# Mod jobs one turn later, fetches and exponentials in another order, and Hyena's inverse transform folded over even and odd times

## The chip, the cores and the metric

One NeuronCore of a Trainium2 chip runs the whole program. The metric is device microseconds of one execution, median of several runs. TensorE does the matrix products; VectorE, ScalarE and GpSimd (called Pool) run beside it, and the SyncE and Pool queues start the DMA transfers. Engines wait for each other through counting semaphores.

## The reference, cut to what matters

A two-layer diffusion backbone on 256 latent tokens of width 1024 with 256 context tokens. Layer 0 mixes with neighbourhood attention and a short convolution, layer 1 with a Hyena long convolution. Each layer has a SwiGLU FFN before and after the mixer, and each sub-layer takes shift, scale and gate from `silu(c) @ w_mod`.

```python
def half_step_ffn(x, g_pre, g_post, shift, scale, gate, w_gate, w_up, w_down):
    h = modulated_norm(x, g_pre, shift, scale)
    y = (jax.nn.silu(h @ w_gate) * (h @ w_up)) @ w_down
    return x + FFN_RES * gate * rms_norm(y, g_post)

def bidirectional_long_conv(u, h_fwd, h_bwd):
    n = u.shape[1]
    k = jnp.concatenate([h_fwd, jnp.zeros((1, HY_WIDTH), jnp.float32), h_bwd[1:][::-1]], axis=0)
    u_f = jnp.fft.rfft(u.astype(jnp.float32), n=2 * n, axis=1)
    k_f = jnp.fft.rfft(k, n=2 * n, axis=0)
    y = jnp.fft.irfft(u_f * k_f[None], n=2 * n, axis=1)[:, :n]
    return y.astype(u.dtype)

# hyena_mixer
    x0, x1, v = jnp.split(short_conv(h @ w_in, short_w), 3, axis=-1)
    u = v * x1
    return (x0 * (bidirectional_long_conv(u, h_fwd, h_bwd) + u * bias)) @ w_out
```

Sizes: D = 1024, D_FF = 2816, 256 tokens, depth 2.

## The kernel before

Every engine has a program of its own, written out by hand, and its order is the order of that text.

**Weights.** The stream `wstream` is cut into units of 128x1024 f32 (512 KB), fetched by SyncE into a ring of six slots. ScalarE rounds a unit to `whi` (`split_hi`, L652), VectorE subtracts to get `wlo_r` (`split`, L1106), four units ahead of TensorE (LEAD = 4). A product is three matmuls: hi by hi, lo by hi, hi by lo (L1798 to L1800 with columns, L1879 to L1881 in down projections).

**FFN.** There are four, numbered 0 to 3; FFN 0 carries the context tokens too. Each has 11 turns of six units: gate and up of pair 0 (k = 0, 1), gate and up of pair 1 (k = 2, 3), two down units (k = 4, 5). After unit 1 and after unit 3 ScalarE takes `silu` (L789), VectorE multiplies (`gate_up`, L1323) and makes `act_lo` (`act_los`, L1328), for which the down units wait. Turns are written out, except for ranges in `LOOPS`, which are loops. `at_steps` puts other calls at a turn and a k.

**Jobs.** The modulation `silu(c) @ w_mod` runs as jobs on VectorE beside the FFN turns: eight multiply-adds of 128x512 (`job_ops`, L1121, L1123), a hi part by ScalarE (`job_hi`), a lo part (`job_lo`, L1133), and in the turn after it two matmuls by TensorE (`job_sum`). FFN 1 has six jobs, FFN 2 eight, FFN 3 two. Pool fetches their 2 MB in four parts (`load_job`), each after the multiply-adds that free its place (`steps_before`). `batch_rows`, `batch_columns` and `batch_out` turn the finished rows into columns; `gate_out` finishes a gate.

**Start.** The first four loads of `w_mod` (16 chunks) are computed ahead on TensorE: `chunk_hi` by ScalarE (L880), `chunk_lo` by VectorE (L1442), `ahead` by TensorE (L1991, L1993; L1984 for load 3), then `row` (L888), `ahead_columns` (L2002) and `ahead_out` (L1153). `warm_bank` issues matmuls of the identity whose result nobody reads (L1972).

**Filters.** In turns 6 to 10 of FFN 1 Hyena's filters are made: `filter_layer`, `sine_argument` (L1658 to L1668 on VectorE), `sine` on ScalarE, `filter_out`, `filter_sums`. They need `w4`, `window` and `bias_row`; the transforms after FFN 1 need `dft`.

**Attention.** Projection units 0 to 23 (`take_out`, L943 to L948 on ScalarE; `short_conv`, L1511 to L1522 on VectorE), beside them the context's norm (`spread`, L1190 and L1216; its transposes L1865 stand behind unit 9). Then per head: `score`, `maxima` (L1531), `exps` (L984), `normalise` (L1561, L1563), transposes (L2199), copies to `prob_t` (L1006), `values` (L2187).

**Hyena.** Projection units 0 to 23: ScalarE takes a tap (L1071), VectorE the two others (`taps`, L1731, L1734), then a split, then what stands in the tables. The spectrum of `u` comes from TensorE (`u_spectrum`, L2324); `spectrum_product` multiplies it on VectorE in `YF_STEPS` steps for each half g of the channels, placed by `YF_AT` (unit to list of (g, step)). `yf_step` counts the steps. The inverse transform (`inverse`, L2337) takes the 128 channels of chunk c: four f32 matmuls of 256 columns, each in two records. Inverses 0 to 3 stand behind projection units 19 to 22 (`IV_AT`), inverses 4 to 7 behind units 1 to 4 of the output projection (`IV_UNITS`). Inverses 0 and 4 wait for all steps of their half. `inverse_out` (L1745, L1747) and `mixed_hi` (L1063) follow.

## Time and profile before

| what | us |
|---|---|
| median of 3 runs | 1323.95 (1320.19 to 1324.26) |
| profiled execution | 1324.37 |
| its span, first to last instruction | 1322.7 |
| TensorE busy | 1292.2 (98%) |
| VectorE busy | 988.4 (75%) |
| ScalarE busy | 637.8 (48%) |
| granted TensorE clock, mean | 0.995 |

Stages in the profiled execution, from its timeline: start 0 to 60, FFN 0 to 368 with the context's down projection to 434, attention to 581, FFN 1 from 589, FFN 2 from 801, Hyena from 1003, FFN 3 from 1128, end at 1322.7. Times below are microseconds from the start of the span. A line of the timeline or chain starts with its start and its length; `xN` is a count of instructions; in brackets stands how long the engine had been idle and what ended it. A matmul's end is modelled, about 0.28 to 0.40 after its start, while the next one starts 0.117 (256 columns of f32r) or 0.235 (512) after it.

### The profile page before, as it was taken

How to read it: one execution, taken by the hardware profiler on the slowest of the kernel's cores; microseconds unless marked ns; L12 is line 12 of the kernel's file. 1: busy time of each engine (PE TensorE's matmuls, PEld its weight loads, DVE VectorE, ACT ScalarE, POOL GpSimd, SP SyncE). 2: the span in 40 equal slices, each digit the busy share in tenths (PEclk: the TensorE clock that was granted, in tenths of full speed). 3: DMA queues.
4: the chain of work that ended last, by engine and by line, in shares of the span. 5: the costliest groups of instructions: out<-in, count | busy, mean ns of one | idle time of the engine just before them, and what ended most of it. 6: DMA issues, size and time to landing. Idle time of an engine off the chain costs nothing.

```text
span 1322.7 us, 21457 instructions
## 1 busy us (share of the span) xinstructions
PE 1292.2 (98%) x7746; PEld 1111.7 (84%) x7746; DVE 988.4 (75%) x1459; ACT 637.8 (48%) x1011; POOL 119.9 (9%) x211
## 2 busy tenths in 40 slices
PE   7999999999999999999999999999999999999998
PEld 5678777887778998688998888989998988999997
DVE  5688777788786886758786768888768887965554
ACT  6533333233376665765444447444447434644444
POOL 2100010111100422011110000111000000000000
PEclk9999999999999999999999999999999999999999
DMA  9655657777755754259886546898654536656553
GB/s 357 210 175 177 203 203 241 257 240 254 242 172 177 221 145 110 81 178 335 286 303 203 176 145 207 303 354 287 215 182 142 159 125 205 222 180 189 184 184 109
DMA packets 76474, 275.67 MB, mean 208 GB/s; under 512 B 9274, under 2 KB 9829, under 8 KB 75760
## 3 DMA queue, kind: packets, MB, share of 16 engines
q1 hardware_dynamic: 52128, 187.00, 43.5%
q0 software_dynamic: 24272, 87.65, 19.6%
q8 instruction: 50, 0.82, 0.2%
q14 instruction: 24, 0.20, 0.1%
HBM read 273.57 MB, written 1.05 MB: 208 GB/s over the span
## 4 chain that ended last, share of the span: by engine, by line
PE 80%; DVE 9%; ACT 5%; DMA 3%; issue 2%; POOL 0%; DVEq 0%; ACTq 0%; SPq 0%; POOLq 0%
PE gu L1798 16%; PE gu L1800 16%; PE gu L1799 15%; PE acc L1879 8%; PE acc L1881 8%; PE acc L1880 8%; DVE wlo_r L1106 3%; DMA area<-in_wmod_dram 2%; DMA wlo<-in_wstream_dram 1%; ACT whi L652 1%; DVE part L1123 1%; DVE x_lat L1307 1%; PE acc L2164 1%; PE acc L2166 1%; PE acc L2165 1%
## 5 line engine op out<-in xcount | busy, mean ns | idle before, releaser
L1798 PE MATMUL gu<-h_hi,whi 128*128 128x256 f32 (+1 forms) x1664 | 510.6, 307 | 2.2 <-ACT area L948 1.2
L1800 PE MATMUL gu<-h_hi,wlo_r 128*128 128x256 f32 (+1 forms) x1664 | 507.6, 305 | 0.0
L1799 PE MATMUL gu<-h_lo,whi 128*128 128x256 f32 (+1 forms) x1664 | 507.4, 305 | 0.0
L1106 DVE TENSOR_TENSOR wlo_r<-wlo,whi 128x1024 fp32r<-128x1024 f32 x350 | 420.9, 1222 | 84.5 <-ACT whi L652 82.4
L652 ACT ACTIVATE whi<-wlo 128x1024 fp32r<-128x1024 f32 x350 | 360.7, 1050 | 81.0 <-DMA wlo<-in_wstream_dram 80.6
L1798 PEld LDWEIGHTS gu<-h_hi,whi 128*128 128x128 f32 x1664 | 313.4, 188 | 26.5 <-issue 4.5
L1799 PEld LDWEIGHTS gu<-h_lo,whi 128*128 128x128 f32 x1664 | 313.3, 188 | 18.9 <-issue 0.7
L1800 PEld LDWEIGHTS gu<-h_hi,wlo_r 128*128 128x128 f32 x1664 | 313.9, 189 | 15.7
L1123 DVE SCALAR_TENSOR_TENSOR part<-wm,cvec,part 128x512 f32<-128x512 f32 x266 | 199.4, 750 | 7.0 <-DVE part L1123 0.5
L1879 PE MATMUL acc<-whi,act_hi 128*128 128x512 f32 x440 | 177.6, 404 | 5.6 <-DVE act_lo L1328 5.1
L1881 PE MATMUL acc<-wlo_r,act_hi 128*128 128x512 f32 x440 | 174.0, 396 | 0.0
L1880 PE MATMUL acc<-whi,act_lo 128*128 128x512 f32 x440 | 174.0, 395 | 0.0
L546 POOL DMA_DIRECT2D wm<-in_wmod_dram x128 | 68.0, 532 | 749.6 <-DVE part L1123 576.0
L1879 PEld LDWEIGHTS acc<-whi,act_hi 128*128 128x128 f32 x440 | 82.9, 188 | 30.1 <-DVE act_lo L1328 8.1
L789 ACT ACTIVATE gated<-gu 128x256 f32<-128x256 f32 x66 | 25.3, 383 | 171.0 <-PE gu L1800 171.0
L1881 PEld LDWEIGHTS acc<-wlo_r,act_hi 128*128 128x128 f32 x440 | 83.0, 189 | 20.9
L1880 PEld LDWEIGHTS acc<-whi,act_lo 128*128 128x128 f32 x440 | 83.1, 189 | 17.5
L1323 DVE TENSOR_TENSOR act<-gated,gu 128x256 f32<-128x256 f32 x66 | 27.7, 420 | 80.7 <-ACT gated L789 80.6
L786 ACT ACTIVATE total_hi<-part 128x512 fp32r<-128x512 f32 x38 | 24.0, 632 | 78.9 <-DVE part L1123 78.6
L847 ACT ACTIVATE act_hi<-act 128x256 fp32r<-128x256 f32 x22 | 9.2, 418 | 104.1 <-DVE act L1415 104.1
L1328 DVE TENSOR_TENSOR act_lo<-act,act_hi 128x256 fp32r<-128x256 f32 x88 | 37.2, 423 | 20.4 <-ACT act_hi L793 16.4
L793 ACT ACTIVATE act_hi<-act 128x256 fp32r<-128x256 f32 x66 | 27.6, 418 | 48.7 <-DVE act L1323 48.7
(375 smaller groups left out, 1251.1 us busy)
## 6 DMA issues: line engine op xcount, KB each, us to landing
wlo<-in_wstream_dram SPq DMA_DIRECT2D x350, 512.0 KB, 3.6
wm<-in_wmod_dram POOLq DMA_DIRECT2D x132, 512.0 KB, 5.6
area<-in_wmod_dram POOLq DMA_DIRECT2D x11, 512.0 KB, 19.9
z<-in_gate_rows_dram POOLq DMA_DIRECT2D x6, 512.0 KB, 9.6
gate_keep<-in_gate_rows_dram POOLq DMA_DIRECT2D x5, 512.0 KB, 8.0
area<-in_rpb_dram POOLq DMA_DIRECT2D x32, 64.0 KB, 3.5
x_lat<-in_x_in_dram SPq DMA_DIRECT2D x1, 1024.0 KB, 7.8
area<-in_ctx_in_dram SPq DMA_DIRECT2D x1, 1024.0 KB, 9.0
```

The lines of the kernel that those rows point to most:

```text
L546: pool.dma_start(wm[:, 2 * part_:2 * part_ + 2, :], src[:, 2 * part_:2 * part_ + 2, :]).then_inc(wm_landed[part_ // 2], 16)
L652: nc.scalar.activation(whi[:, phase % RING, :], raw[:, phase % RING, :], ACT.Copy).then_inc(hi_done, 1)
L1106: nc.vector.tensor_tensor(wlo[:, u.base % RING, :], raw[:, u.base % RING, :], whi[:, u.base % RING, :].bitcast(F32), ALU.subtract).then_in ...
L1123: ins = nc.vector.scalar_tensor_tensor(out=part[:, :], in0=wm[:, kt, :], scalar=c, in1=part[:, :], op0=ALU.mult, op1=ALU.add)
L1323: nc.vector.tensor_tensor(dst, gated[:, s, :], gu[:, s, T:2 * T], ALU.mult).then_inc(act_mul, 1)
L1328: nc.vector.tensor_tensor(act_lo[:, s, :], act[:, s, :], act_hi[:, s, :].bitcast(F32), ALU.subtract).then_inc(act_lo_done, 1)
L1798: nc.tensor.matmul(out_, w_hi, x_hi, start=start, stop=False, skip_group_check=True)
L1799: nc.tensor.matmul(out_, w_hi, x_lo, start=False, stop=False, skip_group_check=True)
L1800: return nc.tensor.matmul(out_, w_lo, x_hi, start=False, stop=stop, skip_group_check=True)
L1879: nc.tensor.matmul(y, x_hi[:, tok], whi[:, s, cols], start=kt_first, stop=False, skip_group_check=True)
L1880: nc.tensor.matmul(y, x_lo[:, tok], whi[:, s, cols], start=False, stop=False, skip_group_check=True)
L1881: ins = nc.tensor.matmul(y, x_hi[:, tok], wlo[:, s, cols], start=False, stop=kt_last, skip_group_check=True)
```

## The change

- Jobs of FFN 1, 2 and 3 run one turn later (`JOB_TURN`), with the loops, the batch steps and the gates that hang on them. 
- Pool's fetches after attention: job loads are mixed with `w4`, `window`, `bias_row` and `dft`, and in FFN 2 with the gate and gain rows, one after each job load.
- Start: 23 warming matmuls in place of 16 (`EARLY`), nine later ones without the wait for `xt_copied` in place of eight with it, and two new ones ahead of `ahead_columns(1)`. ScalarE's `row(1)` goes ahead of `chunk_hi(10)`.
- Attention: `exps(4)` and `exps(6)` go ahead of the copies of heads 2 and 4; `spread` of the context norm goes from units 5 and 6 to 7 and 8.
- Hyena: two more spectrum steps for each half, a sum and a scaled difference of the spectra's low and high bins. The inverse makes even and odd times apart, each from two products of 128 columns. `inverse_out` puts them in order while it multiplies. ScalarE's second copy of odd spectra waits for step 7 in place of 8.

```diff
-LOOPS = [{3: 6}, {2: 6}, {2: 4}, {3: 10}]
+LOOPS = [{3: 6}, {3: 6}, {3: 5}, {4: 10}]
+JOB_TURN = [0, 1, 1, 1]
...
-            pool.dma_start(dft, dft_in).then_inc(dft_landed, 16)
+            for l in (JOB_L[1] + 1, JOB_L[1] + 2):
+                load_job(l, gemv, steps_before(l))
             for rows_ in (slice(0, HY_FFN), slice(HY_FFN, 2 * HY_FFN)):
                 pool.dma_start(w4[rows_, :], fw4).then_inc(filt_in, 16)
+            load_job(JOB_L[1] + 3, gemv, steps_before(JOB_L[1] + 3))
             pool.dma_start(window, window_in).then_inc(filt_in, 16)
...
-            with pool.Fori(JOB_L[1] + 1, JOB_L[2] + 1) as l:
+            load_job(JOB_L[1] + 4, gemv, steps_before(JOB_L[1] + 4))
+            pool.dma_start(dft, dft_in).then_inc(dft_landed, 16)
+            with pool.Fori(JOB_L[1] + 5, JOB_L[2] + 1) as l:
                 load_job(l, gemv, steps_before(l))
-            with pool.Fori(JOB_L[2] + 1, JOB_L[2] + 4) as l:
-                load_job(l, gemv, steps_before(l))
-            for b in (2, 5):
-                load_gate(1, b)
-                load_gain(1, b)
-            with pool.Fori(JOB_L[2] + 4, JOB_L[3]) as l:
+            for l, load_row, b in ((1, load_gate, 2), (2, load_gain, 2), (3, load_gate, 5), (4, load_gain, 5)):
+                load_job(JOB_L[2] + l, gemv, steps_before(JOB_L[2] + l))
+                load_row(1, b)
+            with pool.Fori(JOB_L[2] + 5, JOB_L[3]) as l:
                 load_job(l, gemv, steps_before(l))
...
-            for n in (8, 9, 10):
+            for n in (8, 9):
                 chunk_hi(n)
             row(1)
-            chunk_hi(11)
+            for n in (10, 11):
+                chunk_hi(n)
...
             for h in range(HEADS):
+                if h in (2, 4):
+                    exps(h + 2)
                 for t in range(2):
...
-                if h + 2 < HEADS:
+                if h + 2 < HEADS and h not in (2, 4):
                     exps(h + 2)
...
-            ffn(1, peeled=at_steps([(6, 4)] + SINE_AT + [(7, 5)], [lambda: batch_rows(1)]
+            ffn(1, peeled=at_steps([(7, 1)] + SINE_AT + [(7, 5)], [lambda: batch_rows(1)]
...
-                        a.wait_ge(yf_step, YF_STEPS)
+                        a.wait_ge(yf_step, 7)
...
-                      5: lambda: spread(5, 0), 6: lambda: spread(5, 1), 9: lambda: h_los(5, (0, 1)),
+                      7: lambda: spread(5, 0), 8: lambda: spread(5, 1), 9: lambda: h_los(5, (0, 1)),
...
-                nc.vector.tensor_tensor(conv[:, c % 4, :], inverse_bank(c), x0[:, c, :], ALU.mult).then_inc(inv_step, 1)
+                nc.vector.tensor_tensor(by_parity(conv[:, c % 4, :]), inverse_bank(c).rearrange("p (a n) -> p a n", a=2),
+                                        by_parity(x0[:, c, :]), ALU.mult).then_inc(inv_step, 1)
...
+                elif step_ >= 8:
+                    v.wait_ge(yf_step, YF_STEPS * g + step_)
+                    low, high = y_f[:, 0::2, cols], y_f[:, 1::2, cols]
+                    if step_ == 8:
+                        nc.vector.tensor_tensor(low, low, high, ALU.add).then_inc(yf_step, 1)
+                    else:
+                        nc.vector.scalar_tensor_tensor(out=high, in0=high, scalar=-2.0, in1=low, op0=ALU.mult,
+                                                       op1=ALU.add).then_inc(yf_step, 1)
...
-            pe.wait_ge(xt_copied, 4)
-            warm_bank(8, acc[:, 3, 0:P])
+            warm_bank(9, mean_p[:, 0:P])
...
             norm_columns(1, 1)
+            warm_bank(2, gu[:, 1, 0:P])
             ahead_columns(1)
...
-            ffn(1, 4, peeled=at_steps([(7, 0)] + FILTER_AT, [lambda: batch_columns(1)]
+            ffn(1, 4, peeled=at_steps([(7, 3)] + FILTER_AT, [lambda: batch_columns(1)]
...
-                for k in range(4):
-                    ins = nc.tensor.matmul(inverse_bank(c), y_f[:, k, c * P:(c + 1) * P], dft[:, 4 + k, :], start=(k == 0),
-                                           stop=(k == 3))
+                for odd in range(2):
+                    times = slice(odd * P, odd * P + P)
+                    for n, (k, table) in enumerate(((odd, 4), (3 - odd, 6))):
+                        ins = nc.tensor.matmul(inverse_bank(c)[:, times], y_f[:, k, c * P:(c + 1) * P], dft[:, table, times],
+                                               start=(n == 0), stop=(n == 1))
...
-EARLY = 16
+EARLY = 23
...
-ROWS_AT, BATCH_AT, COEF_AT = (4, 2), (4, 4), (5, 0)
+ROWS_AT, BATCH_AT, COEF_AT = (5, 2), (5, 4), (6, 0)
...
-YF_AT = {12: [(0, 0)], 13: [(0, 1)], 14: [(0, 2)], 15: [(0, 3)], 16: [(0, 4), (0, 5)], 17: [(0, 6)], 18: [(0, 7)],
-         19: [(1, 0), (1, 1)], 20: [(1, 2)], 21: [(1, 3), (1, 4), (1, 5)], 22: [(1, 6), (1, 7)]}
-YF_STEPS = 8
+YF_AT = {12: [(0, 0)], 13: [(0, 1)], 14: [(0, 2)], 15: [(0, 3)], 16: [(0, 4), (0, 5)], 17: [(0, 6), (0, 7)],
+         18: [(0, 8), (0, 9)], 19: [(1, 0), (1, 1)], 20: [(1, 2)], 21: [(1, 3), (1, 4), (1, 5)], 22: [(1, 6), (1, 7)],
+         23: [(1, 8), (1, 9)]}
+YF_STEPS = 10
...
-    dft = np.stack([cos[times], sin[times], cos.T / T, sin.T / T]).astype(f).reshape(8, P, T).transpose(1, 0, 2)
+    dft = np.stack([cos[times], sin[times], cos.T[:, times] / T, sin.T[:, times] / T]).astype(f).reshape(8, P, T).transpose(1, 0, 2)
```

The rest of the diff carries `JOB_TURN` through `ffn` of ScalarE, VectorE and TensorE: turn i runs job i - 1.

## Rows read from the trace of the kernel before

**Rows 1.** The page's first section: busy time, share of the span, instructions.
```profile
PE 1292.2 (98%) x7746; PEld 1111.7 (84%) x7746; DVE 988.4 (75%) x1459; ACT 637.8 (48%) x1011; POOL 119.9 (9%) x211
```

**Rows 2.** Chain of work in the start: start, length, what.
```profile
6.77 22.19 DMA area<-in_wmod_dram
...
29.95 0.58 ACT row_sb L888
...
30.57 1.81 PE mean_p L2002 x8
...
33.33 0.43 PE job_p L1991
...
38.53 3.52 PE mean_p L1984 x8
```

**Rows 3.** Stretches: length, busy by engine, granted clock (PEclk), DMA share, GB/s.
```profile
27.20:30.60 3.40, 2.01 (x17) 1.76 (x17) 1.83 (x3) 1.66 (x4) 0.00 (x0) 1.00 1.03 412
30.70:37.40 6.70, 6.70 (x21) 3.05 (x22) 4.92 (x13) 3.16 (x6) 1.80 (x4) 0.50 0.55 179
606.30:624.00 17.70, 15.57 (x113) 13.95 (x112) 13.87 (x20) 8.84 (x12) 1.59 (x3) 1.00 0.97 354
624.60:627.90 3.30, 3.30 (x9) 2.60 (x8) 3.30 (x5) 2.67 (x4) 0.53 (x1) 0.50 0.78 230
```

**Rows 4.** Timeline of TensorE: waits in FFN 1, 2 and 3.
```profile
606.99 0.36 PE L1798 MATMUL gu<-h_hi,whi 128*128 128x256 f32 x1 [0.27 <-DVE wlo_r L1106]
...
623.80 0.49 PE L1879 MATMUL acc<-whi,act_hi 128*128 128x512 f32 x1 [1.85 <-DVE act_lo L1328]
...
816.82 0.50 PE L1879 MATMUL acc<-whi,act_hi 128*128 128x512 f32 x1 [0.92 <-DVE act_lo L1328]
...
869.93 0.50 PE L1879 MATMUL acc<-whi,act_hi 128*128 128x512 f32 x1 [0.67 <-DVE act_lo L1328]
...
1142.53 0.50 PE L1879 MATMUL acc<-whi,act_hi 128*128 128x512 f32 x1 [0.49 <-DVE act_lo L1328]
```

**Rows 5.** Timeline of VectorE in FFN 1: a job turn, and turn 6.
```profile
634.99 0.42 DVE L1323 TENSOR_TENSOR act<-gated,gu 128x256 f32<-128x256 f32 x1 [3.38 <-ACT gated L789]
...
640.66 0.42 DVE L1323 TENSOR_TENSOR act<-gated,gu 128x256 f32<-128x256 f32 x1 [0.54 <-ACT gated L789]
...
708.67 0.53 DVE L1658 TENSOR_SCALAR area<-mean_p,area 64x256 f32<-64x256 f32 x1
...
711.44 0.41 DVE L1323 TENSOR_TENSOR act<-gated,gu 128x256 f32<-128x256 f32 x1
```

**Rows 6.** Timeline of TensorE in the attention projection and in the heads.
```profile
460.70 0.39 PE L1798 MATMUL gu<-h_hi,whi 128*128 128x256 f32 x1 [0.95 <-ACT area L948]
...
551.61 0.33 PE L2199 MATMUL acc<-ident,area 128*128 128x128 f32 x1 [1.41 <-DVE area L1563]
```

**Rows 7.** Timeline of VectorE in Hyena's projection.
```profile
1071.67 1.22 DVE L1766 TENSOR_TENSOR area<-area,wm 128x1024 f32<-128x1024 f32 x1
1074.40 0.48 DVE L1731 SCALAR_TENSOR_TENSOR area<-gu,sm,area 128x255 f32<-128x255 f32 x1 [1.52 <-ACT area L1071]
...
1093.72 2.35 DVE L1766 TENSOR_TENSOR area<-area,wm 128x1024 f32<-128x1024 f32 x2
...
1098.29 3.50 DVE L1106 TENSOR_TENSOR wlo_r<-wlo,whi 128x1024 fp32r<-128x1024 f32 x3
```

**Rows 8.** Timeline of TensorE: warming matmuls, and inverses 0 and 4.
```profile
581.68 3.73 PE L1972 MATMUL gu<-ident 128*128 128x128 f32 x32
...
1072.94 1.99 PE L2337 MATMUL job_p<-area 128*128 128x256 f32 x8 [0.19 <-DVE area L1766]
...
1096.71 1.89 PE L2337 MATMUL job_p<-area 128*128 128x256 f32 x8
1098.25 0.58 PE L1879 MATMUL acc<-whi,h_hi 128*128 128x512 f32 x1
```

**Rows 9.** Groups by shape on VectorE: a scaled difference of 1024 elements.
```profile
L1715 DVE SCALAR_TENSOR_TENSOR area<-area 128x1024 f32<-128x1024 f32 x2 | 2.4, 1220 | 0.0
```

More of the change, by code:

```diff
@@ L854, in ffn @@
             def ffn(f, peeled={}):
-                t0, jobs = JOB_0[f], len(JOBS[f])
+                turn0, jobs = JOB_TURN[f], len(JOBS[f])
+                t0 = JOB_0[f] - turn0
                 for i, end in turns_of(f):
@@ L858, in ffn @@
                         ffn_turn(Unit(U_FFN[f] + 6 * i), PAIR0[f] + 2 * i, between=peeled.get(i, {}), last=i == FH - 1,
-                                 t=t0 + i if i < jobs else None, first=i == 0)
+                                 t=t0 + i if 0 <= i - turn0 < jobs else None, first=i == 0)
                     else:
                         with a.Fori(i, end) as j:
-                            ffn_turn(Unit(U_FFN[f], j), j * 2 + PAIR0[f], t=j + t0 if i < jobs else None)
+                            ffn_turn(Unit(U_FFN[f], j), j * 2 + PAIR0[f], t=j + t0 if 0 <= i - turn0 < jobs else None)
             def batch_rows(b):
@@ L1339, in ffn_turn @@
                 i = n - n0 if isinstance(n, int) else None
-                before = JOBS[f][i // 2 - 1] if i is not None and 0 < i // 2 <= len(JOBS[f]) else None
+                past = i // 2 - 1 - JOB_TURN[f] if i is not None else -1
+                before = JOBS[f][past] if 0 <= past < len(JOBS[f]) else None
                 for k in range(6):
@@ L1354, in ffn_turn @@
                     if k == 1 and before is not None and is_gate(before):
-                        gate_out(JOB_0[f] + i // 2 - 1, before)
+                        gate_out(JOB_0[f] + past, before)
                     if k == 4 and job is not None:
@@ L1366, in ffn @@
                 n0, a0, t0, l0, jobs = PAIR0[f], ACT0[f], JOB_0[f], JOB_L[f], len(JOBS[f])
+                turn0 = JOB_TURN[f]
                 def job(i):
-                    row_ = i if not isinstance(i, int) else None if is_gate(JOBS[f][i]) else job_row(JOBS[f][i])
-                    return (i + t0, row_, i * 32 + 32 * (l0 - 3))
+                    row_ = i - turn0 if not isinstance(i, int) else None if is_gate(JOBS[f][i - turn0]) else job_row(JOBS[f][i - turn0])
+                    return (i + (t0 - turn0), row_, i * 32 + 32 * (l0 - 3 - turn0))
                 for i, end in turns_of(f):
                     if end is None:
-                        ffn_turn(f, Unit(U_FFN[f] + 6 * i), n0 + 2 * i, a0 + 2 * i, job(i) if i < jobs else None,
+                        ffn_turn(f, Unit(U_FFN[f] + 6 * i), n0 + 2 * i, a0 + 2 * i, job(i) if 0 <= i - turn0 < jobs else None,
                                  peeled.get(i, {}), i == FH - 1, i == 0)
@@ L1377, in ffn @@
                         with v.Fori(i, end) as j:
-                            ffn_turn(f, Unit(U_FFN[f], j), j * 2 + n0, j * 2 + a0, job(j) if i < jobs else None)
+                            ffn_turn(f, Unit(U_FFN[f], j), j * 2 + n0, j * 2 + a0, job(j) if 0 <= i - turn0 < jobs else None)
             def context_los(ft, s):
@@ L1738, in taps, with by_parity @@
                     nc.vector.tensor_tensor(u_t[:, idx // 2, :], conv[:, (idx - 1) % 4, :], c, ALU.mult).then_inc(hy_step, 1)
+            def by_parity(x_):
+                return x_.rearrange("p (n a) -> p a n", a=2)
             def inverse_out(c):
@@ L1958, in ffn @@
                 xs = (late_hi, late_lo)
-                n0, a0, t0, u0, jobs = PAIR0[f], ACT0[f], JOB_0[f], U_FFN[f], len(JOBS[f])
+                n0, a0, u0, jobs = PAIR0[f], ACT0[f], U_FFN[f], len(JOBS[f])
+                past = 1 + JOB_TURN[f]
+                t0 = JOB_0[f] - past
                 for i, end in turns_of(f):
                     if end is None:
-                        ffn_turn(Unit(u0 + 6 * i), n0 + 2 * i, a0 + 2 * i, (t0 + i - 1, JOBS[f][i - 1], i == 1) if 0 < i <= jobs else None, xs, i == 0,
+                        ffn_turn(Unit(u0 + 6 * i), n0 + 2 * i, a0 + 2 * i, (t0 + i, JOBS[f][i - past], i == past) if 0 <= i - past < jobs else None, xs, i == 0,
                                  8 * p if i == 0 else None, i == FH - 1, peeled.get(i, {}), bank_free if i == 0 else None)
@@ L1965, in ffn @@
                         with pe.Fori(i, end) as j:
-                            ffn_turn(Unit(u0, j), j * 2 + n0, j * 2 + a0, (j + (t0 - 1), None) if i <= jobs else None, xs)
+                            ffn_turn(Unit(u0, j), j * 2 + n0, j * 2 + a0, (j + t0, None) if 0 < i - past < jobs else None, xs)
             def warm_bank(n, out_):
```

## The prediction

> **What bounds the kernel now.** I read the page first. TensorE is busy for 98% of the span [rows 1], so time goes only where work is taken off TensorE or where TensorE stands still, and where VectorE makes it stand still. Then I looked for TensorE's waits in its timeline, stage by stage, and for the granted clock beside them. Four places carry the argument. In the start the chain runs through a landing chunk, a copy `row_sb` by ScalarE and eight two-column matmuls [rows 2]; just there the clock falls to half for 6.8 us [rows 3]. In the first turns of the three later FFNs TensorE waits for VectorE's `act_lo`, and once, at 623.8, the clock falls again behind it [rows 3, 4]. In turn 6 of FFN 1 VectorE has to take a sine argument between two activations [rows 5]. In the Hyena input projection VectorE works without a pause and the spectrum steps (L1757 to L1766) feed the inverse transform just in time [rows 7, 8]. I date everything by the profiled execution: span 1322.7, run 1324.37, which is 0.42 above the median 1323.95.
>
> **Start.** `row(1)` (L888) was issued behind `chunk_hi(10)`, which waited for its landing until 28.96; the copy ran at 29.95 and TensorE idled 1.39 us before `ahead_columns(1)` at 30.57 [rows 2]. Now row 1 is copied before chunk 10: its own conditions are met by 28.2, so it is done by 28.8, and TensorE goes from the transposes through two warming matmuls (4 records of 0.117 [rows 8], 0.5 us) into the columns at about 29.65. That is 0.9 us earlier. If the clock then stays up, the 16 matmuls of `ahead(2)` are 0.235 apart instead of 0.43 [rows 2], the eight column matmuls take about 1.0 for 1.8, and the stretch that ended at 38.5 ends at about 34.5. Chunk 11 doesn't hold it up: VectorE's split of it ends near 32.7, needed at 33.5. The next chunks land at 412 GB/s, the rate of the stretch around them [rows 3], the last near 35.3, needed at 39. So -3.9 with the clock held, -0.8 with the same fall. Against the gain: the stretch before the fall held two-column matmuls, transposes and the idle time, and TensorE was busy 2.01 of 3.4 us there [rows 3]; only the idle part is closed. I take -3.9 as likelier. The 23 early warming matmuls fill 8.9 to 10.2, where TensorE waited anyway; nine instead of eight later ones no longer wait for the copies and end ahead of the chunk they precede: 0.
>
> **FFN 1, 2 and 3: jobs one turn later.** A job costs VectorE 0.5 + 7 x 0.75 + 0.7 + 0.2, about 6.5 us. The norm ahead leaves VectorE late in turn 0; without a job there it catches up. In FFN 1 this comes with 3.1 MB (`dft`, `window`, `w4`) no longer queued at once at 588. Stretch 606.3 to 624.0 has 15.57 us of work in 17.70 (2.1 lost) and the next 3.3 us run at half clock (1.7 lost) [rows 3]; a gap at 606.7 [rows 4] and one of its kind at 603.2 add about 1.0 from start to start. A gap is really 0.16 longer than printed, since a matmul's end stands 0.40 behind its start though the next starts 0.235 behind it. I take -4.8. FFN 2 has 0.92 at 816.8, 0.67 at 869.9 and a small one at 812.8; the second follows four row loads (2.1 MB) at once, which are now spread one to a job. FFN 3 has 0.49 [rows 4]. With the 0.16 each, about -2.3 and -0.7: -3.0 together. What comes next in each is VectorE's normal turn, which has an idle place of about 3.4 us and one of 0.54 [rows 5].
>
> Where the job goes it costs something once. Turn 6 of FFN 1 now has the last job and the sine argument of layer 0 (708.67 to 711.44, 2.8 us [rows 5]) between the activation of pair 0 and that of pair 1. In a job turn this stretch has 0.54 us to spare. The second activation comes 2.3 us late; TensorE's own filter matmuls in between give 0.7 and the lead of `act_lo` over its use 0.8: +0.8 (0 to +1.7). Turn 7 takes the rest in its idle place. The job loads on Pool's queue now wait behind one another's VectorE steps with `w4`, `window` and `dft` behind loads 22, 23 and 24: turns 2 to 4 move 12 x 0.524 = 6.3 MB in 17.4 us, 361 GB/s, and the filter's first use is turn 6. The trace moves 412 GB/s in the start [rows 3], so 0 (0 to +1). The Trainium skill, "DMA: Bandwidth & Descriptors", section "Where 436 GB/s comes from", puts the limit from device memory near 358 GB/s for a core; by it each of these turns would be 0.2 us too full, +0.6 in all. The row contradicts it here. Instruction fetch for one more written-out turn: no row shows a price; 0, and at most the 0.5 that I add to the upper end.
>
> **Attention and its projection.** In the projection `spread` moves from units 5, 6 to 7, 8. The wait of 0.95 at 460.7 [rows 6] goes, as `short_conv(0)` comes 0.9 earlier. But the transposes behind unit 9 now need a scaling that ends near 464.9 (split, 0.95, split, 0.95 behind 461), and TensorE is there at 463.7: it waits about 1.4 in two steps. Net +0.5 (-0.9 to +1). For heads 2 and 4 the exponentials go ahead of the copies. The wait of 1.41 at 551.6 ends with VectorE's normalising [rows 6], which stands behind the maxima of head 7, themselves behind the last scores; the exponentials were done before that. 0 (-0.5 to +0.5, the copies of head 2 come 1 us later).
>
> **Hyena's inverse.** Work on TensorE halves: 8 chunks of 8 records (an f32 matmul has two), 256 columns at 0.216, become 64 records of 128 columns. From start to the next unit a chunk took 1.54 (1096.71 to 1098.25); with 0.117 a record [rows 8] it takes 0.9. 8 x 0.63 = -5.0. VectorE gets four new operations of 1024 elements, 1.22 each for a sum and for a scaled difference [rows 7, 9], two to a half of the channels, and each inverse waits for all ten steps of its half. Both are on the path:
> First half. Step 7 is issued one unit earlier; then taps, split, steps 8 and 9. From 1072.89 (end of 1071.67) the last step moves by 2.4 to about 1075.3. ScalarE's copy now waits for step 7 only, so the 1.52 idle before the taps at 1074.40 goes [rows 7]; VectorE leaves 0.96 late instead of 2.4. TensorE starts inverse 0 2.4 late; with 0.63 back in each of four inverses it is even by inverse 4 (reached at 1096.5, for 1096.71).
> Second half. The last step ended about 1096 and inverse 4 was issued at 1096.71 with no wait [rows 7, 8]. Now, 0.96 late, VectorE does `inverse_out(3)`, the taps and split of unit 23 (1098.29 + 1.1 + 0.96 = 1100.4), then steps 8 and 9: 1100.4 + 1.2 + 1.3 = 1102.9. TensorE stands from 1096.5 to 1102.9, 6.4 us, for nothing else is in its order there. Unit 2 of the output projection starts at 1103.8 instead of 1098.25: +5.6; three inverses are left at 0.63: +3.7. `inverse_out` 4 to 7 follow in time. A wait of 1.85 was followed by about 3.3 us of half clock [rows 3, 4], so I add 1.7 for the same behind this one (0 if it falls and rises in the wait, 3.4 as at the start).
> The strided `inverse_out` (every other element) has no row; nearest is the contiguous one, 0.42 [rows 7]. I take 0, and +0.4 for each of the first four at the upper end. The Trainium skill, "SBUF — State Buffer", section "Door 1: The DMA port swizzle", says that two f32 in a line of 16 bytes still run at full rate; by it the term is 0, no run here shows it.
> Hyena: +3.7 + 1.7 = +5.4.
>
> **Sum.** -3.9 - 4.8 - 3.0 + 0.8 + 0.5 + 5.4 = -5.0. 1324.37 - 5.0 = 1319.4, 4.6 (0.34%) under the median. A measurement tells 0.3%, 4 us, from no change.
>
> **Rivals.**
> Inverse gain in full: VectorE has time, so TensorE doesn't wait at inverse 4. Then -5.0 instead of +5.4: 1309.0. For it: VectorE is busy 75% in all [rows 1]. Against: around 1070 to 1100 its rows follow each other without a gap but for those that wait for ScalarE.
> Start as before: the clock falls again near 30. 1319.4 + 3.1 = 1322.5. For it: the stretch still consists of small work.
> It doesn't do what it says in FFN 1 and 2: VectorE is late in turn 0 from the norm alone, and the waits only move to turn 1. 1319.4 + 4.8 = 1324.2.
> Slower: Pool's transfers crowd the weights' in turns 2 to 4 of FFN 1, as in turns 0 and 1 now. The place is the `act_lo` wait of each turn, the price that of the stretch at 606 to 628, 2.1 + 1.7, for three turns 11.4: 1330.8. It decides when a weight unit lands later than the lead that ScalarE and VectorE have over TensorE, four units of 2.85 us less a split on each, about 9 us. For it: 361 GB/s over a whole turn. Against: 412 GB/s reached, and only 1 MB at a time.
>
> **How the numbers follow.** Forecast 0.52, inverse gain in full 0.12, start as before 0.14, waits only moved 0.10, crowded turns 0.12. The forecast's own unknowns (clock behind the Hyena wait, turn 6, `spread`, strides) make it 1316 to 1323; seven tenths of it lie below 1319.98, the bound for faster. Faster 0.12 + 0.36 + 0.02 = 0.50, same 0.16 + 0.12 + 0.10 = 0.38, slower 0.12. The range 1308 to 1326 leaves the crowded turns out.
>
> **What would show it.** TensorE's timeline shows a wait of about 6 us ahead of the fifth inverse, ended by VectorE's scaled difference, and one of 2 to 3 us ahead of the first; the two-record groups of 128 columns are 0.11 apart. The clock is whole from the first warming to the Hyena wait. `act_lo` waits in turns 0 and 1 are gone, and one of about 0.8 stands in turn 6 of FFN 1. If there is no wait before inverse 4, or the start falls to half again, or wm landings lag in turns 2 to 4, the prediction is wrong in that term.

## The result, and the profile after

The changed kernel takes 1325.04 us (median of 20 runs, 1323.42 to 1327.72), the kernel before 1322.80 beside it (20 runs, 1316.53 to 1325.83). The ratio is 1.0023, with a 95% interval of 1.0014 to 1.0031: slower by 2 to 4 us, where 4.6 us less had been forecast. The profiled execution took 1324.74 us with a span of 1323.0, close to its median; that of before (1324.37) had been 1.6 above the median of its twenty.

The first table lays the two profiled executions side by side, by the start of the same matmul in each (behind the start, the last transpose of the norm ahead of each stage).

| stretch | before | after | difference | forecast |
|---|---|---|---|---|
| start, to the second unit of FFN 0 | 58.98 | 54.99 | -3.99 | -3.9 |
| FFN 0 and attention, to FFN 1 | 529.18 | 529.40 | +0.22 | +0.5 |
| FFN 1 | 212.15 | 214.39 | +2.24 | -4.8 + 0.8 |
| FFN 2 | 202.07 | 200.07 | -2.00 | -2.3 |
| Hyena and its norm | 124.66 | 129.26 | +4.60 | +5.4 |
| FFN 3 to the end | 195.66 | 194.89 | -0.77 | -0.7 |
| span | 1322.70 | 1323.00 | +0.30 | -5.0 |

One line is clearly wrong, FFN 1's, by 6.2 us. The page's busy times, beside [rows 1]:

```profile
PE 1288.3 (97%) x7766; PEld 1111.1 (84%) x7766; DVE 993.3 (75%) x1463; ACT 638.7 (48%) x1011; POOL 119.6 (9%) x211
```

TensorE has 3.9 us less to do and a span that is no shorter. VectorE has 4.9 us more: the four new operations.

**Start**, for [rows 2, 3]: ScalarE's copy, TensorE's warming and columns, and the stretch that was at half clock.

```profile
28.39 0.59 ACT L892 ACTIVATE row_sb<-mean_p 4x512 f32<-4x512 f32 x1
```

```profile
29.16 0.61 PE L1997 MATMUL gu<-ident 128*128 128x128 f32 x4
29.70 1.05 PE L2027 MATMUL mean_p<-pick,row_sb 4*128 4x2 f32 x8
```

```profile
30.70:37.40 6.70, 6.70 (x24) 1.84 (x24) 5.87 (x15) 4.11 (x8) 2.04 (x4) 1.00 0.58 196
```

The copy no longer stands behind chunk 10, nothing is idle ahead of the columns, and the granted clock is 1.00 where it was 0.50.

**FFN 1, turn 3.** The chain of waits, ScalarE's timeline, TensorE's, and two stretches (length, busy by engine, granted clock, DMA share, GB/s):

```profile
639.54 11.99 DMA wlo<-in_wstream_dram
```

```profile
649.00 1.06 ACT L655 ACTIVATE whi<-wlo 128x1024 fp32r<-128x1024 f32 x1 [5.02 <-DMA wlo<-in_wstream_dram]
651.55 1.06 ACT L655 ACTIVATE whi<-wlo 128x1024 fp32r<-128x1024 f32 x1 [1.49 <-DMA wlo<-in_wstream_dram]
```

```profile
655.33 0.49 PE L1902 MATMUL acc<-whi,act_hi 128*128 128x512 f32 x1 [4.19 <-DVE act_lo L1335]
```

```profile
636.00:650.00 14.00, 14.00 (x109) 13.38 (x108) 7.47 (x11) 3.70 (x5) 1.45 (x3) 1.00 1.01 289
...
656.10:659.40 3.30, 3.30 (x9) 2.57 (x8) 3.30 (x5) 2.72 (x4) 1.54 (x3) 0.50 0.88 258
```

TensorE's wait is put down to `act_lo`, but VectorE had been idle too. One step up the chain, ScalarE waited 5.02 us for one weight unit and 1.49 for the next; each took about 12 us from issue to landing (the first row is the second of them). The DMA engines are full (share 1.01) and yet move only 289 GB/s; in the start a full stretch moved 412 [rows 3]. The waits of turns 0 and 1 [rows 4] are gone.

**Hyena**, for [rows 7, 8]: the last scaled difference of each half, a strided `inverse_out`, inverses 0, 1 and 4, and the two stretches at half clock.

```profile
1070.55 1.23 DVE L1784 SCALAR_TENSOR_TENSOR area<-area 128x1024 f32<-128x1024 f32 x1
...
1076.13 0.41 DVE L1759 TENSOR_TENSOR area<-job_p,area 128x256 f32<-128x256 f32 x1
...
1098.49 1.23 DVE L1784 SCALAR_TENSOR_TENSOR area<-area 128x1024 f32<-128x1024 f32 x1
```

```profile
1071.83 1.51 PE L2364 MATMUL job_p<-area 128*128 128x128 f32 x8 [2.59 <-DVE area L1784]
1077.21 1.05 PE L2364 MATMUL mean_p<-area 128*128 128x128 f32 x8
...
1099.77 2.08 PE L2364 MATMUL job_p<-area 128*128 128x128 f32 x8 [5.79 <-DVE area L1784]
```

```profile
1072.60:1075.80 3.20, 3.20 (x17) 3.20 (x17) 3.17 (x4) 0.00 (x0) 0.00 (x0) 0.50 0.00 1
...
1096.50:1103.10 6.60, 3.33 (x12) 3.05 (x13) 6.08 (x7) 2.11 (x4) 0.00 (x0) 0.50 0.08 32
```

Both waits stand where the forecast put them, both ended by the scaled difference, and the strided product costs the same 0.41 as the contiguous one.

### The profile page after: what moved, and what is told of

The parts are those of the page before. It is cut to its first block, busy times and chain, and to the rows that moved or that the text cites. A ratio compares the mean times of both kernels' runs of the same rounds, so it can differ in the third digit from the quotient of the medians.

```text
span 1323.0 us, 21321 instructions
## 1 busy us (share of the span) xinstructions
PE 1288.3 (97%) x7766; PEld 1111.1 (84%) x7766; DVE 993.3 (75%) x1463; ACT 638.7 (48%) x1011; POOL 119.6 (9%) x211
## 4 chain that ended last, share of the span: by engine, by line
PE 80%; DVE 11%; ACT 5%; DMA 2%; issue 2%; DVEq 0%; SPq 0%; ACTq 0%
PE gu L1821 15%; PE gu L1823 15%; PE gu L1822 15%; PE acc L1902 8%; PE acc L1904 8%; PE acc L1903 8%; DVE wlo_r L1113 2%; DMA wlo<-in_wstream_dram 2%; ACT whi L655 1%; DMA x_lat<-in_x_in_dram 1%; DVE wlo_r L1452 1%; DVE part L1130 1%; DVE x_lat L1314 1%; PE acc L2189 1%; PE acc L2190 1%
```

## The experiments

The theory after the result: two causes, w4 in turn 3 of FFN 1 (about 6 us) and Hyena's steps 8 and 9 on VectorE (about 5), against gains in the start, FFN 2 and FFN 3. Its rivals are named in each expectation. Times are medians; ratios are against the kernel before on the same chip. The groups e1 to e4, e5 to e8, e9 to e12 and e13 with e14 each had the kernel before beside them (1323.03, 1322.07, 1323.42 and 1322.74), so kernels of different groups are better compared by their ratios. The spans are each of one execution.

| kernel | us | ratio, 95% interval | span: FFN 1 | FFN 2 | Hyena |
|---|---|---|---|---|---|
| before, profiled first | 1322.80 | 1 | 212.15 | 202.07 | 124.66 |
| changed | 1325.04 | 1.0023 (1.0014 to 1.0031) | 214.39 | 200.07 | 129.26 |
| e1_full_inverse | 1319.51 | 0.9980 (0.9969 to 0.9991) | 214.21 | 200.06 | 124.33 |
| e2_w4_one | 1343.82 | 1.0159 (1.0138 to 1.0180) | 233.69 | 200.05 | 129.20 |
| e3_w4_early | 1319.49 | 0.9980 (0.9969 to 0.9990) | 209.12 | 200.05 | 129.35 |
| e4_before_again | 1322.52 | 1.0001 (0.9987 to 1.0015) | 210.50 | 203.17 | 124.64 |
| e5_w4_twice | 1320.33 | 0.9984 (0.9973 to 0.9994) | 210.63 | 200.04 | 129.74 |
| e6_steps_first | 1313.84 | 0.9939 (0.9926 to 0.9953) | 208.23 | 200.05 | 123.15 |
| e7_inverse_later | 1316.25 | 0.9955 (0.9941 to 0.9968) | 209.65 | 200.04 | 124.07 |
| e8_both_undone | 1314.97 | 0.9946 (0.9932 to 0.9960) | 210.02 | 200.07 | 124.32 |
| e9_start_only | 1319.01 | 0.9972 (0.9962 to 0.9981) | 212.25 | 203.65 | 124.68 |
| e10_spread_back | 1314.73 | 0.9944 (0.9931 to 0.9957) | 209.56 | 200.02 | 124.31 |
| e11_out_first | 1314.81 | 0.9943 (0.9929 to 0.9957) | 209.96 | 200.05 | 125.07 |
| e12_before_w4_twice | 1318.58 | 0.9975 (0.9964 to 0.9985) | 207.84 | 201.85 | 124.63 |
| e13_start_w4_twice | 1315.97 | 0.9953 (0.9936 to 0.9969) | 207.84 | 202.53 | 124.66 |
| e14_e6_w4_twice | 1313.46 | 0.9938 (0.9919 to 0.9956) | 209.16 | 200.11 | 123.13 |

**e1_full_inverse** undoes Hyena's part alone:

```diff
-                for odd in range(2):
-                    times = slice(odd * P, odd * P + P)
-                    for n, (k, table) in enumerate(((odd, 4), (3 - odd, 6))):
+                for k in range(4):
...
-YF_STEPS = 10
+YF_STEPS = 8
...
```

> The changed kernel with Hyena's inverse as before (four matmuls of 256 columns over all bins, eight spectrum steps), all else as changed. Theory: the new inverse costs what the two traces show between the start of Hyena's projection and the norm behind it, 4.9 us (waits of 2.75 ahead of inverse 0 and 5.95 ahead of inverse 4, half clock behind the second, against 5.0 of matmul time saved). Then this kernel is 4.9 below the changed one: 1320.1, ratio to the kernel before 0.998. Rival: only the profiled execution shows that, and the inverse is neutral: 1325.

1319.51, 5.5 below the changed kernel; its Hyena stretch is 4.9 shorter. The rival falls. The wait in turn 3 is kept (3.36 us in this execution), and FFN 1 is as long as in the changed kernel, 214.21 for 214.39: the two causes are apart.

**e3_w4_early** moves w4 back to where the kernel before has it:

```diff
-            for l in (JOB_L[1] + 1, JOB_L[1] + 2):
-                load_job(l, gemv, steps_before(l))
             for rows_ in (slice(0, HY_FFN), slice(HY_FFN, 2 * HY_FFN)):
                 pool.dma_start(w4[rows_, :], fw4).then_inc(filt_in, 16)
+            for l in (JOB_L[1] + 1, JOB_L[1] + 2):
+                load_job(l, gemv, steps_before(l))
```

> The changed kernel, but both transfers of w4 stand ahead of the two first later job loads, where the kernel before had them (about 588). Theory A: the wait of 4.2 us at 651 and its half clock are gone, and turns 0 and 1 hold, since the window and dft are still spread: 1319 (6.0 below the changed kernel). Rival B: the load crowds turn 0 instead, w4 ahead of two job loads gives a wait of 1 to 2 us with half clock there: 1322 to 1325.

1319.49, 5.5 below the changed kernel. No wait in turns 0 to 3; 1.0 in turn 5 and 0.7 in turn 6 are left. FFN 1 is 5.3 shorter (209.12 for 214.39): the 1 MB of w4 in turn 3 was worth the whole loss there. w4 is as slow as ever at its early place, but nothing is waiting for it.

**e5_w4_twice** leaves w4 in turn 3 but lets it fill all partitions at once:

```diff
-            for rows_ in (slice(0, HY_FFN), slice(HY_FFN, 2 * HY_FFN)):
-                pool.dma_start(w4[rows_, :], fw4).then_inc(filt_in, 16)
+            pool.dma_start(w4, fw4).then_inc(filt_in, 16)
...
-            "fw4": hy_f_w4[0], "fcols": fcols, **constants()}
+            "fw4": np.concatenate([hy_f_w4[0], hy_f_w4[0]]), "fcols": fcols, **constants()}
```

> The changed kernel, w4 at its changed place, but laid out twice in device memory, so that one transfer of 128 rows of 8192 bytes fills all 128 partitions (in the changed kernel two transfers of 64 rows fill 64 partitions each). Same bytes, same place in the queue, no source read with an outer dimension of two. Theory A: what makes w4 dear is that each of its transfers writes 64 partitions (574 to 628 ns a packet, against 310 to 342 for the window and dft). Then its packets take about 340 ns, the load costs 2.7 us of all engines for 4.6, the wait in turn 3 of FFN 1 falls from 4.2 to 1.5 to 2.5 us, and the time to 1321 to 1323. Rival B: the bytes of the turn alone make it; packets stay above 500 ns and the wait at 4 us: 1325.

1320.33, and the wait of turn 3 is nearly gone; one of 1.66 us stands in turn 4, with the clock whole behind it. The same stretch, TensorE's two waits, and w4's row of the DMA issues (KB each, median us to landing), then that row of the changed kernel:

```profile
636.00:650.00 14.00, 14.00 (x110) 13.34 (x109) 10.05 (x14) 5.03 (x7) 1.06 (x2) 1.00 1.02 393
```

```profile
651.27 0.49 PE L1901 MATMUL acc<-whi,act_hi 128*128 128x512 f32 x1 [0.20 <-DVE act_lo L1334]
...
670.57 0.49 PE L1901 MATMUL acc<-whi,act_hi 128*128 128x512 f32 x1 [1.66 <-DVE act_lo L1334]
```

```profile
area<-in_fw_dram POOLq DMA_DIRECT2D x1, 1024.0 KB, 9.4
```

```profile
area<-in_fw_dram POOLq DMA_DIRECT2D x2, 512.0 KB, 11.8
```

Same bytes, same place, same DMA share: 393 GB/s for 289. The trace's DMA records show where the rate went, as the mean time of one packet of 8192 bytes:

```
w4, two transfers of 64 partitions, changed kernel, 642 to 648.5   574 ns
w4, the same with hardly anything beside it, e3, 585 to 592        628 ns
w4, one transfer of 128 partitions, e5, 636 to 648.5               309 ns
window or dft, 128 partitions, changed kernel, 660 to 684          310 to 342 ns
```

It isn't the other queues, since it is slowest where no weight moves beside it (e3, 585.5 to 591). e5 also reads each row of w4 from a place of its own, where the two transfers read the same 0.5 MB; but of the changed kernel's 128 packets the first 64 by start took 564 ns each and the last 64 the same, so a second reading isn't what is slow. What is left is the partitions: a transfer that fills 64 of them ran at about half the rate, and held the engines meanwhile. 128 packets x (574 - 310) ns / 16 = 2.1 us of all engines are lost in a turn of 17.4 us that was nearly full. The expectation was right in kind and too careful in size. Of the 5.5 us that w4's place had cost by e3, 4.7 went with the rate; the rest, with the wait in turn 4, is within what two medians can tell. The Trainium skill, "SBUF — State Buffer", section "Door 1: The DMA port swizzle (why `[64,N]` ≈ `[32,N]`)", says it plainly: partitions 0 to 63 reach 8 of the 16 ports, so 64 partitions move no faster than 32. Its section "Can I just issue two DMAs to hit both halves?" adds that two transfers to the two halves hardly add up. The trace agrees with both, with 574 ns for 309.

**e2_w4_one** meant to test the same without a second copy in memory, by reading the source twice:

```diff
-            for rows_ in (slice(0, HY_FFN), slice(HY_FFN, 2 * HY_FFN)):
-                pool.dma_start(w4[rows_, :], fw4).then_inc(filt_in, 16)
+            pool.dma_start(w4, bass.AP(fw4.tensor, fw4.offset, [[0, 2], [2 * D, HY_FFN], [1, 2 * D]])).then_inc(filt_in, 16)
```

> The changed kernel, but the filter's last weights w4 arrive in one transfer over 128 partitions (source read twice) in place of two over 64 partitions each, at the same place in Pool's queue. Theory A: in turn 3 of FFN 1 the two transfers over 64 partitions hold the DMA engines longer than their bytes (a packet of 8192 bytes took 574 ns there, a packet of the same size of the window 342 ns), so the weight stream lands late and TensorE waits 4.2 us with half clock behind it, 6.0 together. In one transfer the packets take about 340 ns, the load is done 1.9 us sooner, and the wait in turn 3 falls from 4.2 to about 2 with little or no half clock: 1321 to 1323. Rival B: it is the bytes alone (4.7 MB in the turn), so the packets are as slow as before and the wait stays: 1325.

1343.82: neither theory. Its w4 took 32 us to land, and TensorE waited twice. By each wait lies a stretch in which all engines together moved little: 61 GB/s from 655 to 660, 53 from 680 to 684. Its two waits, then w4's row of the issues:

```profile
658.66 0.79 PE L1901 MATMUL acc<-whi,act_hi 128*128 128x512 f32 x1 [7.44 <-DVE act_lo L1334]
...
688.27 0.79 PE L1901 MATMUL acc<-whi,act_hi 128*128 128x512 f32 x1 [13.20 <-DVE act_lo L1334]
```

```profile
area<-in_fw_dram POOLq DMA_DIRECT2D x1, 1024.0 KB, 32.1
```

An engine moves 8192 bytes in 310 ns, 26 GB/s; 53 is two of them. An estimate from these figures: two engines carried w4 and fell behind, and the packets of the other transfers on those two came late. The Trainium skill, "DMA: Bandwidth & Descriptors", section "Rules for kernel authors", has the rule: an outermost dimension of c < 16, such as a repeated read, confines a transfer to c engines. The trace agrees. Of the 64 partitions this kernel says nothing; e5 is that test.

**e4_before_again** is the kernel before, profiled once more.

> The kernel before, profiled again. Theory A: its waits of 1.85 at 623.8 with 3.4 us of half clock behind, and the fall of the clock at 30.7, are not in every execution: the profiled one was 1.6 above the median of twenty, and here one of the two is smaller or missing, with a mean clock above 0.995. Rival B: they are in each, and then the same lines stand here within 0.1 us.

```profile
30.70:37.40 6.70, 6.68 (x25) 2.63 (x26) 5.51 (x14) 3.92 (x7) 1.63 (x4) 0.75 0.54 190
621.80:625.20 3.40, 3.40 (x21) 2.95 (x20) 3.40 (x5) 2.74 (x4) 0.54 (x2) 1.00 0.80 253
```

The waits of FFN 1 are all there (2.02 from start to start in turn 1: the time between two starts less the usual 0.235), but the clock fell for half as long in the start and not at all in FFN 1. So theory A holds: of the 5.1 us that half clock cost the profiled execution, 3.4 weren't in this one.

**e9_start_only** changes the start of the kernel before and nothing else.

```diff
-            for n in (8, 9, 10):
+            for n in (8, 9):
                 chunk_hi(n)
             row(1)
-            chunk_hi(11)
+            for n in (10, 11):
+                chunk_hi(n)
...
-            pe.wait_ge(xt_copied, 4)
-            warm_bank(8, acc[:, 3, 0:P])
+            warm_bank(9, mean_p[:, 0:P])
...
+            warm_bank(2, gu[:, 1, 0:P])
...
-EARLY = 16
+EARLY = 23
```

> The kernel before with the start alone changed (row 1 ahead of chunk 10, 23 early warming matmuls for 16, nine later ones that wait for nothing, two ahead of the columns). Theory A: 0.9 of the idle time goes in every execution, and the fall of the clock behind it goes too, which cost 3.1 us in one profiled execution of before (half for 6.8 us) and 1.6 in the other (half for 3.4): -2.5 to -4 against the median of before, 1319 to 1320. Rival B: the start moves against FFN 1's or attention's waits, which absorb it: 1322.

1319.01, -4.4, by the ratio -3.7. The clock stays whole:

```profile
30.70:37.40 6.70, 6.70 (x24) 1.74 (x22) 5.87 (x14) 4.08 (x7) 1.64 (x4) 1.00 0.46 171
```

That holds further: in all 13 profiled executions with the new start no half clock shows before FFN 1, and in all three with the old one it does (6.8 us, then 3.4 in e4 and 3.4 in e12). What of the start holds it, the order of the copy or the warming matmuls, no run separates.

**e8_both_undone** puts e1 and e3 together.

> The changed kernel with w4 early and with Hyena's inverse as before: what is left is the start, the order of spread and exponentials, and the jobs one turn later. Theory: the two causes add, 1325.0 - 5.5 - 5.5 = 1314.0, and neither has a wait of over 1.2 us from FFN 1 to the end. Rival: they overlap somewhere (the stream of weights, the clock), 1316 or more.

1314.97: the two causes add. From e9 to here, everything that is left (jobs, order of the fetches, spread, exponentials) brings 4.0, by the ratios 3.4.

**e12_before_w4_twice** gives the kernel before the one full transfer of w4 (with `fw4` laid out twice, as in e5), its jobs and all else in place.

```diff
-            for rows_ in (slice(0, HY_FFN), slice(HY_FFN, 2 * HY_FFN)):
-                pool.dma_start(w4[rows_, :], fw4).then_inc(filt_in, 16)
+            pool.dma_start(w4, fw4).then_inc(filt_in, 16)
...
```

> The kernel before with w4 as one transfer of 128 rows, at its place at 588. Theory A: the waits of FFN 1's turns 0 and 1 in the kernel before (0.63, 0.44 and 2.02 from start to start) come from weights that land late behind the burst, of which w4 has 4.6 us at half speed; with 2.6 for them the wait of 2.02 falls to 0 to 1: 1320.5 to 1322. Rival B (the one of the prediction): VectorE is late from the norm and the job, and the waits stay as they are: 1322.5.

1318.58, -4.8, by the ratio -3.3 (-1.9 to -4.8). The stretch 590 to 600 in it, then in the kernel before, which is there 2.7 us behind (592.7 to 602.7 moved 285 GB/s), with ScalarE's timeline of the latter:

```profile
590.00:600.00 10.00, 10.00 (x76) 9.54 (x76) 9.64 (x15) 5.94 (x10) 1.08 (x2) 1.00 1.01 412
```

```profile
590.00:600.00 10.00, 10.00 (x88) 10.00 (x87) 9.47 (x17) 8.17 (x15) 1.50 (x3) 1.00 0.98 276
```

```profile
606.98 1.06 ACT L652 ACTIVATE whi<-wlo 128x1024 fp32r<-128x1024 f32 x1 [1.39 <-DMA wlo<-in_wstream_dram]
609.54 1.06 ACT L652 ACTIVATE whi<-wlo 128x1024 fp32r<-128x1024 f32 x1 [0.98 <-DMA wlo<-in_wstream_dram]
612.07 1.06 ACT L652 ACTIVATE whi<-wlo 128x1024 fp32r<-128x1024 f32 x1 [1.47 <-DMA wlo<-in_wstream_dram]
```

The job stands in turn 0 as before, and of the three waits there only the first, 0.47 at 600.91, is left. So the wait of 1.85 at 623.8 hangs on weights that landed 2.5 us apart behind the same slow w4. VectorE is a link of that chain: behind the last late unit, which landed 11.2 us after its issue at 603.36, it makes up the splits and the job's multiply-adds, and `act_lo` comes at 623.33. Rival B, the prediction's own reading, falls for this wait and holds for the one at 600.91. The job has its share all the same: in e3, where w4 is early and slow (628 ns a packet) but the job is out of turn 0 and `dft` and the window are out of the queue, all three waits are gone as well. So the late weights and the job make the 1.85 together; no run moves the jobs alone.

**e13_start_w4_twice** is e9 with e12's w4.

> The kernel before with the start changed as in e9_start_only and w4 as one transfer of 128 rows at its place at 588; jobs where they were. Theory A: the moved jobs only avoided the burst that w4 lengthened in FFN 1, and bring 2 us in FFN 2 (rows loaded four at once) and 0.8 in FFN 3. Then FFN 1's stretch from the norm's last transposes to the next norm's takes 208 us as in e12_before_w4_twice (209 to 210 with the jobs moved and w4 early), and the whole is 1318.6 - 4.0 = 1314.6, the same as e8_both_undone (1315.0). Rival B: VectorE's lateness from the norm matters by itself, and this kernel is 2 us or more behind e8: 1317.

1315.97, between the two expectations. FFN 1 takes 207.84 with the jobs where they were, against 208.2 to 210.0 with the jobs moved and w4 early. e8 is 1.0 ahead in the medians (the ratios' intervals overlap), by FFN 2 (200.07 for 202.53) and FFN 3 (194.88 for 195.76) in the profiles. With w4 at full rate the moved jobs bring nothing in FFN 1 but cost about 1 us: e14 takes 209.16, by the waits in turns 4, 5 and 6. In FFN 2 the change brings 2 to 3 us, and in FFN 3 mostly 0.8. In FFN 2 the jobs and the spread of the row loads are not separated, but a wait in its turn 0 (0.91 to 0.92 us, the one at 816.8 [rows 4]) stands in all five profiled executions with the jobs in their old turns, whatever w4 does, and in none with them moved.

**e6_steps_first** has w4 early and another order in Hyena:

```diff
-IV_AT = {19: 0, 20: 1, 21: 2, 22: 3}
+IV_AT = {20: 0, 21: 1, 22: 2, 23: 3}
...
-21: [(1, 3), (1, 4), (1, 5)], 22: [(1, 6), (1, 7)],
-         23: [(1, 8), (1, 9)]}
+21: [(1, 3), (1, 4), (1, 5)], 22: [(1, 6), (1, 7), (1, 8), (1, 9)]}
```

> w4 early as in e3_w4_early (1319.5), and in Hyena steps 8 and 9 of the second half right behind step 7 (after unit 22, ahead of unit 23's taps and split), and inverses 0 to 3 one unit later (after units 20 to 23). Theory: VectorE's order alone sets both waits. The one ahead of inverse 0 (2.75) goes, as VectorE has a unit more; the last step ends about 2.4 us plus one split and taps earlier, 3.5 in all, so unit 2 of the output projection starts 3 to 4 earlier, and the wait ahead of inverse 4 is 4 to 5: 1316. Rival: the late taps of unit 23 and its split become the new wait (TensorE waits for the split of the output projection's first units) and half of it is lost: 1318.

1313.84, 5.7 below e3, more than expected: the wait ahead of inverse 4 is gone, not shortened. The steps' place and the inverses' later units changed together; no run separates them. VectorE's timeline and TensorE's:

```profile
1087.44 1.22 DVE L1784 SCALAR_TENSOR_TENSOR area<-area 128x1024 f32<-128x1024 f32 x1
```

```profile
1080.82 1.27 PE L2364 MATMUL mean_p<-area 128*128 128x128 f32 x8 [1.92 <-DVE area L1759]
...
1089.15 1.13 PE L2364 MATMUL job_p<-area 128*128 128x128 f32 x8
```

The last difference ends at 1088.66, 0.5 ahead of inverse 4. What is left is inverse 3, which waits for `inverse_out(1)` behind three spectrum steps, with half clock for 3.4 us behind it. Hyena is now 1.2 shorter than with the whole inverse.

**e7_inverse_later** and **e11_out_first** try for that rest.

```diff
-IV_UNITS = {1: 4, 2: 5, 3: 6, 4: 7}
+IV_UNITS = {2: (4,), 3: (5,), 4: (6, 7)}
```

> e6_steps_first, and inverses 4 and 5 one unit of the output projection later, with 6 and 7 both after unit 4. Theory: the unit of 2.85 us fills the wait ahead of inverse 4, which falls from 4 to 5 us to 1 to 2, with no half clock behind it; about 1 us comes back ahead of the last unit, which needs inverse 7: 1313. Rival: the wait only moves to the last unit, 3 us there: 1315.

e11 adds to this (and puts `spread` back):

```diff
+                if idx in IV_AT:
+                    inverse_out(IV_AT[idx])
                 for g, step_ in YF_AT.get(idx, ()):
                     spectrum_product(g, step_)
-                if idx in IV_AT:
-                    inverse_out(IV_AT[idx])
```

> e7_inverse_later, with spread back and with inverse_out ahead of the spectrum steps in VectorE's order of units 20 to 23. Theory: inverse 3 waited 1.9 us for inverse_out(1), which stood behind three spectrum steps, and half clock followed; both go (3.4), the wait of 1.0 ahead of unit 3 goes, the steps end 0.9 later, which the unit ahead of inverse 4 covers: 1311. Rival: VectorE has no room, the steps end later than TensorE reaches inverse 4 and the wait only moves there: 1314.

1316.25 and 1314.81, both no better than e6. In e7 the wait of inverse 3 stays and unit 3 waits 0.97 more; in e11 inverse 3 is free and the waits stand one and two steps on (e11, TensorE's timeline):

```profile
1090.14 1.16 PE L2364 MATMUL job_p<-area 128*128 128x128 f32 x8 [1.66 <-DVE area L1784]
...
1093.64 0.47 PE L1902 MATMUL acc<-whi,h_hi 128*128 128x512 f32 x1 [2.35 <-DVE h_lo L1762]
```

VectorE bounds this stretch: it is busy for 20.2 of the 22 us from 1070 to 1092 in e11, and these orders only chose where TensorE waits. Why e7's median is 2.4 above its own profiled 1313.88 is not settled.

**e10_spread_back** is e8 with `spread` back beside units 5 and 6.

```diff
-                      7: lambda: spread(5, 0), 8: lambda: spread(5, 1), 9: lambda: h_los(5, (0, 1)),
+                      5: lambda: spread(5, 0), 6: lambda: spread(5, 1), 9: lambda: h_los(5, (0, 1)),
```

> e8_both_undone (1315.0), with spread beside units 5 and 6 as before. The stretch from the FFN 1-like end at 379 to the second unit behind the projection took 96.66 us in four kernels with the moved spread, 96.28 and 95.14 in the two executions of the kernel before. Theory A: the move costs 0.4 to 1.5, and this kernel is at 1313.5 to 1314.6. Rival B: the wait of 0.95 ahead of short_conv's scaling comes in each execution, and it makes no difference: 1315.0.

1314.73 for 1314.97, and ratios whose intervals overlap: no difference that can be told.

**e14_e6_w4_twice** joins e6 and the full transfer.

> e6_steps_first (1313.8) with w4 as one transfer of 128 rows at the early place. Theory: w4 was hidden there already (no wait in FFN 1 but the one of 0.7 in turn 6), so 0 to 0.5 is gained: 1313.5. Rival: at full rate it ends before the weights need the queues, and the waits of 1.0 to 1.5 in turn 5 that some executions had go as well: 1312.5.

1313.46, the same as e6 within their spread. e6 and e14 beat both kernels, by 8 to 9 us (0.6%) against the one before and 11 against the changed one.

## Why the prediction was wrong

**Start: right.** -3.99 in the profiled pair for -3.9 forecast, with the mechanism as told (copy, idle time, clock); e9 confirms it with -3.7 to -4.4. The size has some luck in it: it was worked out against an execution with 6.8 us of half clock. Against e4, with 3.4, the same stretch gained 2.6.

**FFN 1's first turns: wrong in size, and the cause half seen.** "The norm ahead leaves VectorE late in turn 0; without a job there it catches up" fits the wait of 0.47 in turn 0, which e12 leaves in place, and the first waits of FFN 2. It doesn't carry the largest, 1.85 in turn 1: the waits did go, but e12 makes two of the three go with the job in place. Those hung on w4's rate, and I had taken the line that ended the wait (`act_lo`) for its cause without walking further to ScalarE's waits for landings. The prediction does name the 3.1 MB queued at once at 588, but has no price for their rate. The 1.7 of half clock in the sum is one execution's: e4 has none. Measured, the jobs' move with w4 early takes FFN 1 from 210.5 (e4) or 212.15 to 208.2 to 210.0: 0.5 to 3.9, where 4.0 (-4.8 + 0.8) was forecast.

**FFN 1's turns 2 to 4: the step that failed, and that cost the sign.** The prediction put this term at 0 (0 to +1): "6.3 MB in 17.4 us, 361 GB/s ... The trace moves 412 GB/s in the start, so 0". The rate was taken from transfers of 128 partitions and used for one of 64, though the code has both `rows_` halves in plain sight. With 64 partitions a packet took 574 ns for 309, the turn's DMA engines were full at 289 GB/s, and TensorE waited. The forecast's sum lacks +6.0 here: 4.19 (4.36 from start to start) and 1.65 of half clock behind it. The rival "crowded turns" had the place (`act_lo` in turns 2 to 4), the condition (a unit landing later than 9 us; 12 measured) and the wrong price: 11.4 for three turns, where it was one turn with 6.0. Its chance of 0.12 was too small. The limit of device memory that the prediction quotes and sets aside (+0.6) would not have found it either; the limit lay with the partitions.

**Turn 6: right.** A wait of 0.56 at 711.06, 0.72 from start to start, for +0.8.

**Attention: right and small.** A wait of 0.91 at 460.77 in place of 0.95 at 460.70 [rows 6]; +0.22 for +0.5. Of the waits in the heads the one of 1.41 stayed (1.40), as forecast, and one of 0.42 us at 544.59 went; no run changes the exponentials alone. e9 and e13, with attention as before and the new start, take 529.1 and 529.3 for the changed kernel's 529.4.

**FFN 2 and 3: right.** -2.0 and -0.8 for -2.3 and -0.7; against e4, whose wait in turn 3 of FFN 2 was 1.96 from start to start, the gain is 3.1.

**Hyena: right in both mechanisms.** Inverse 0 began 2.4 later in its own terms (1071.83 + 3.51 - 1072.94) for 2.4 forecast, and TensorE waited 5.79 ahead of inverse 4 for 6.4. An inverse fell from 1.54 to 0.81, not 0.9, which gives 0.7 more in all; against it the clock was at half behind the first wait too (1.6), where I had it behind the second only (1.7). Sum +4.95 without the norm, for +5.4.

**The clock's share.** The forecast was dated by an execution that lost 5.1 us to half clock. Its later profile lost 1.7. The changed kernel's execution lost 5.1 as well, behind the wait of turn 3 and both Hyena waits, and its runs lie closer together (4.3 apart for 9.3). Why is not shown: e5, with the same order in Hyena, had no fall at the first wait there and 10.2 us of half clock at the second. That the profiled execution of before was 1.6 above its median and that of the changed kernel 0.3 below is most of why the spans differ by 0.3 and the medians by 2.2.

## What to carry to other kernels

Before a load is moved into a turn that is nearly full, write down not only its bytes but the partitions that each of its transfers fills: here 64 partitions cost nearly double time on all DMA engines, at either place in the queue. When a wait is put down to an engine that was itself idle, follow it until an engine or a transfer is found that worked without a pause, and test that link by itself: e12 changed only the transfer and took away two waits that had been put down to VectorE. A saving on TensorE that adds nearly as much to VectorE just ahead of it (5.8 here against 4.9) pays only if the added steps are placed by the first reader's time: the same operations gave +4.9 in one order and -1.2 in another.

## What the runs showed of the hardware

A packet of 8192 bytes took 574 to 628 ns in a transfer to 64 partitions and 309 in one to 128, with the DMA share at 1.0 in both. A transfer whose source was read twice through an outer dimension of two took 32 us for 1 MB, and in two stretches behind it all engines together moved 53 to 61 GB/s. The granted clock fell behind the same wait of 2.0 us in one execution of the kernel before and not in another.
